# Projections put between the attention's iterations, and a quarter of the U tiles put between the V tiles

## The reference, cut to what matters

```python
(fq, fk, fv, ff, gq, gk, gv, gg, glr, mga, mgb) = jnp.split(x @ w_in, IN_SPLIT_POINTS, axis=-1)
y_fox = fox_attention(fq, fk, fv, ff + bias) @ w_out_fox      # 8 heads of 64, causal, 512 frames
o = gla_chunk_attention(gq, gk, gv, log_sigmoid(glr @ gate_up + gate_bias) / 16)   # 4 heads, chunks of 64
y_gla = (rms_norm(o) * gain * silu(gg)) @ w_out_gla
x = layer_norm(ALPHA * x + (sigmoid(mga) * y_fox + sigmoid(mgb) * y_gla) @ w_out)
# PEER: 8 heads x 16 picks for each of 512 tokens, out of 128 x 128 experts
s_top, i_top = top_k(q . sub_keys, 16)       # two halves, then the best 16 of 16 x 16 pairs
gates = softmax(best)
act = gelu(x . expert_u[picked]);  ffn = sum(act * gates * expert_v[picked])
x = layer_norm(ALPHA * x + ffn)
```

## Time and profile before

| what | value |
|---|---|
| median of three runs | 2075.17 us (2071.8 to 2093.76) |
| profiled execution, own time | 2075.27 us |
| its span, first to last instruction | 2073.5 us |
| mean granted TensorE clock | 0.954 |
| busy over the span: TensorE, VectorE, ScalarE, GpSimd | 97%, 53%, 33%, 45% |
| HBM read, written | 305.96 MB, 60.82 MB |

### The profile page before, as it was taken

How to read it: one execution, slowest core, us unless ns; L and a number is a source line. 1 busy time by engine, 2 the same in 40 slices (tenths; PEclk the granted TensorE clock), 3 DMA queues, 4 the chain that set the end, 5 groups by cost and what they waited for, 6 DMA issues and landing times.

```text
span 2073.5 us, 24488 instructions
## 1 busy us (share of the span) xinstructions
PE 2012.5 (97%) x9433; PEld 1601.0 (77%) x9433; DVE 1096.2 (53%) x2127; ACT 682.6 (33%) x1031; POOL 939.9 (45%) x502
## 2 busy tenths in 40 slices
PE   8999999999989999999999999999997999999998
PEld 5787554788777888888888888888885878787786
DVE  4001223401250199895488888600156878897787
ACT  4632222422213323333333333322332333333332
POOL 6442000344416334445333333344488888888530
PEclk9998558999989999999999999999999999999999
DMA  5221000132324234444456666654477999999983
GB/s 187 92 93 60 1 0 11 61 100 89 130 88 132 82 102 149 141 149 141 145 184 195 193 199 193 194 207 148 141 274 260 353 351 335 371 378 333 401 320 122
DMA packets 164774, 368.38 MB, mean 178 GB/s; under 512 B 15266, under 2 KB 80930, under 8 KB 164531
## 3 DMA queue, kind: packets, MB, share of 16 engines
q1 hardware_dynamic: 51264, 184.57, 25.6%
q10 hardware_dynamic: 90866, 115.06, 16.4%
q0 software_dynamic: 22528, 67.19, 8.8%
HBM read 305.96 MB, written 60.82 MB: 177 GB/s over the span
## 4 chain that ended last, share of the span: by engine, by line
PE 74%; POOL 14%; issue 4%; DVE 4%; DMA 4%; ACT 1%; SPq 0%; ACTq 0%; DVEq 0%
PE bank L403 20%; PE bank L405 20%; PE bank L404 20%; POOL weight L365 8%; POOL gat L373 6%; PE bank L645 3%; DMA act<-activation_scratch 3%; PE bank L496 2%; PE bank L518 2%; PE bank L508 1%; PE bank L533 1%; DVE acc L1110 1%; PE bank L499 1%; PE bank L541 1%; DMA gat<-in_expert_v,eidx 1%
## 5 line engine op out<-in xcount | busy, mean ns | idle before, releaser
L353 POOL TENSOR_TENSOR w_lo<-stage,w_hi 128x1024 fp32r<-128x1024 f32 x224 | 543.5, 2434 | 951.2 <-ACT w_hi L703 951.1
L403 PE MATMUL bank<-x_hi,w_lo 128*128 128x512 f32 x1376 | 543.5, 395 | 6.9 <-DVE x_lo L977 4.4
L405 PE MATMUL bank<-x_hi,w_hi 128*128 128x512 f32 x1376 | 537.7, 391 | 0.0
L404 PE MATMUL bank<-x_lo,w_hi 128*128 128x512 f32 x1376 | 537.2, 390 | 0.0
L703 ACT ACTIVATE w_hi<-stage 128x1024 fp32r<-128x1024 f32 x348 | 358.7, 1041 | 23.4 <-PE bank L405 14.2
L403 PE MATMUL bank<-w_hi,wt_lo 128*128 128x512 f32 x768 | 304.0, 396 | 31.1 <-issue 18.5
L403 PEld LDWEIGHTS bank<-x_hi,w_lo 128*128 128x128 f32 x1376 | 259.4, 189 | 61.1 <-DVE x_lo L977 5.3
L404 PE MATMUL bank<-w_lo,wt_hi 128*128 128x512 f32 x768 | 302.3, 394 | 0.0
L405 PE MATMUL bank<-w_hi,wt_hi 128*128 128x512 f32 x768 | 302.2, 393 | 0.0
L405 PEld LDWEIGHTS bank<-x_hi,w_hi 128*128 128x128 f32 x1376 | 259.3, 188 | 55.4
L404 PEld LDWEIGHTS bank<-x_lo,w_hi 128*128 128x128 f32 x1376 | 259.7, 189 | 52.6 <-issue 0.2
(11 more groups left out here) (214 smaller groups left out, 1983.4 us busy)
## 6 DMA issues: line engine op xcount, KB each, us to landing
stage<-in_expert_uT SPq DMA_DIRECT2D x128, 512.0 KB
stage<-in_expert_v SPq DMA_DIRECT2D x128, 512.0 KB
stage<-in_mix_stream SPq DMA_DIRECT2D x84, 512.0 KB
gates<-gate_scratch ACTq DMA_DIRECT2D x32, 768.0 KB
act<-activation_scratch ACTq DMA_DIRECT2D x32, 768.0 KB
activation_scratch<-act_out_a ACTq DMA_DIRECT2D x64, 256.0 KB, 2.3
activation_scratch<-act_out_b ACTq DMA_DIRECT2D x64, 256.0 KB, 2.3
gate_scratch<-gstage_a ACTq DMA_DIRECT2D x6, 2048.0 KB, 11.4
```

Source lines behind the costliest of these rows:

```text
L353: nc.gpsimd.tensor_tensor(w_lo[:, slot, 0:width], stage[:, slot % STAGE, 0:width], w_hi[:, slot, 0:width], ALU.subtract).then_inc(split_do ...
L403: mm(dst, l_lo, r_hi, start=first, stop=False)
L404: mm(dst, l_hi, r_lo, start=False, stop=False)
L405: return mm(dst, l_hi, r_hi, start=False, stop=last)
```

## The change

Two parts are changed together.

In the diff the stretches are, in this order: the numbers and the order of the stream, the banks, GpSimd's loop over the stream, TensorE's attention loop, `score_unit` and V loop, ScalarE after the U phase, and VectorE's `kdec`.

The projections gk, gq, gv0 and gv1 leave the list of projections. They become 16 pieces of 24 matmuls (`FILL`: four row blocks or columns each), and each attention iteration begins with half a piece, 12 matmuls. The attention's logits then have two banks (0 and 1) and the pieces two (2 and 7). sfx now goes straight into `kdec` through the exponential, and VectorE multiplies gk's pieces into it from PSUM.

The U tiles are in two classes. Tiles 0 to 95 (`EARLY`) are computed as before. Of the last 32, block 0 is computed in the U phase, four tiles at once: x's block 0 is the stationary operand and the four tiles are the 512 moving columns (`score_unit`, eight of them, one after each 12 early tiles). Blocks 1 to 3 of each late tile are computed in the V phase, 24 matmuls of 384 columns, before every fourth V tile; so its tile is streamed a second time. Its activations stay in SBUF (`act_out`) and are multiplied with `late_gates`. V tiles are taken in the order three early, one late. In the V phase GpSimd now makes the low part of each late U tile and of the first of each four V tiles, VectorE that of the other three V tiles. The rows gathered have 5 buffers, not 8, and are written for one tile ahead.

```diff
-GATHER = 8
-EXP_AT = {9: 0, 20: 1, 32: 2, 44: 3}
-TURN_AT = {27: 1, 39: 2, 50: 3}
-FIRST_GATE = 50
-GATE_SPAN = 48
+GATHER = 5
+EARLY = 96
+LATE = NKEY - EARLY
+RUN = EARLY * UNIT // LATE
+EXP_AT = {8: 0, 19: 1, 30: 2, 41: 3}
+TURN_AT = {25: 1, 36: 2, 47: 3}
+FIRST_GATE = 47
+GATE_SPAN = 46
-FIRST_PICK = 10
-LAST_PICK = 118
+FIRST_PICK = 8
+LAST_PICK = 120
...
+def early_place(t):
+    return t + t // RUN * UNIT
+def late_place(m):
+    return NKEY + max(0, 5 * m - 4)
+def value_place(w):
+    return NKEY + 2 + w + min(w // 4, LATE - 2)
+def is_late(w):
+    return w % 4 == 3
-def on_vector(tile):
-    return tile >= NKEY + 4
+def on_vector(place):
+    return place >= NKEY and any(place == value_place(w) for w in range(NKEY) if w % 4 != 0)
...
-        fox_bank = [bank[0], bank[1], bank[2], bank[7]]
+        fox_bank = [bank[0], bank[1]]
+        fill_bank = [bank[2], bank[7]]
-        PT_UNITS = ["fq", "fk", "z", "fv", "gk", "sfx", "gq", "tot", "gv0", "gv1"]
+        PT_UNITS = ["fq", "fk", "z", "fv", "sfx", "tot"]
+        FILL = [("gk", r) for r in range(TB)] + [("gq", r) for r in range(TB)]
+        FILL += [("gv0", r) for r in range(TB)] + [("gv1", r) for r in range(TB)]
...
-            for tile in range(2 * NKEY):
-                n, v = first_expert + tile, tile - NKEY
-                if not on_vector(tile):
-                    split_low(n, n % RING, QW)
-                while acts_due < min(NPICK, 4 * (v - FIRST_PICK + 7), picks_by(v + 3) + 2 * CHUNK_PICKS):
-                while rows_due < picks_by(v + 3):
+            for p in range(len(tiles)):
+                n = first_expert + p
+                if not on_vector(p):
+                    split_low(n, n % RING, QW)
+                w = value_at[p]
+                while acts_due < min(NPICK, 4 * (w - FIRST_PICK + 7), picks_by(w + 1) + 2 * CHUNK_PICKS):
+                while rows_due < picks_by(w + 1):
...
             for i in range(NS + 4):
+                if i < NS:
+                    fill(i)
...
-                    if i >= 4:
-                        pe.wait_ge(fox_exp, i - 3)
-                    L = fox_bank[i % 4]
+                    if i >= 2:
+                        pe.wait_ge(fox_exp, i - 1)
+                    L = fox_bank[i % 2]
...
+            def score_unit(place):
+                n = first_expert + place
+                s = n % RING
+                for k in range(UNIT):
+                    wait_split(pe, n + k)
+                dst = next_out()
+                for c in range(KC):
+                    w = slice(c * P, (c + 1) * P)
+                    ins = mm3(dst[:], x_hi[:, c, 0:P], x_lo[:, c, 0:P], w_hi[:, s:s + UNIT, w], w_lo[:, s:s + UNIT, w],
+                              c == 0, c == KC - 1)
+                ins.then_inc(quarter_used, UNIT)
...
+            score_tile(late_place(0), P)
             for v in range(NKEY - TAIL_TILES):
-                wait_split(pe, first_value + v)
+                if v % 4 == 0:
+                    score_tile(late_place(v // 4 + 1), P)
+                wait_split(pe, first_expert + value_place(v))
...
-                if t == last_group_tile + 2:
-                    load_unit(0)
-                    load_unit(1)
+            for half in range(2):
+                sc.wait_ge(gm_written[half], 16 * NGB // 2)
+            load_unit(0)
+            load_late_gates(0)
+            load_unit(1)
...
-            for r in range(TB):
-                dve.wait_ge(proj_evac, 20 + r + 1)
-                v.tensor_tensor(kdec[:, r, :], kdec[:, r, :], tmp[:, r % 2, :], ALU.mult).then_inc(kdec_ready, 1)
+                if i % 2 == 0 and 0 <= i // 2 - 1 < TB:
+                    r = i // 2 - 1
+                    v.tensor_tensor(kdec[:, r, :], fill_bank[r % 2][:], kdec[:, r, :], ALU.mult).then_inc(kdec_ready, 1)
```

More of the change, by code:

```diff
@@ L253, in build, with fill_quarters_used @@
         first_expert = first_query + HP
-        first_value = first_expert + NKEY
-        PT_UNITS = ["fq", "fk", "z", "fv", "gk", "sfx", "gq", "tot", "gv0", "gv1"]
+        tiles = stream()
+        vector_places = [p for p in range(len(tiles)) if on_vector(p)]
+        PT_UNITS = ["fq", "fk", "z", "fv", "sfx", "tot"]
         AUX = ["z", "sfx", "tot"]
-        STREAMED = [name for name in PT_UNITS if name not in AUX] + ["gg0", "gg1"]
+        FILL = [("gk", r) for r in range(TB)] + [("gq", r) for r in range(TB)]
+        FILL += [("gv0", r) for r in range(TB)] + [("gv1", r) for r in range(TB)]
+        STREAMED = ["fq", "fk", "fv", "gk", "gq", "gv0", "gv1", "gg0", "gg1"]
+        first_fill = 4 * STREAMED.index("gk")
+        def fill_quarters_used(halves):
+            used = 0
+            for h in range(halves):
+                name, r = FILL[h // 2]
+                if name == "gq":
+                    used += h % 2
+                elif r == TB - 1:
+                    used += 2
+            return used
         def wait_product(eng, name, r):
@@ L300, in _ @@
                     m += 1
[L301 to L304, removed]
+            for p, (kind, tile) in enumerate(tiles):
+                load(first_expert + p, expert_uT[tile] if kind == "u" else expert_v[tile])
             for t in range(TB):
@@ L520, in _ @@
                     ins.then_inc(fox_pv, 1)
+            quarter[0] += 16
+            pe.wait_ge(fill_evac, 3 * TB)
             pe.wait_ge(kdec_ready, TB)
@@ L946, in normalize @@
                 act_f(sd[:, t:t + 1], mv[:, t, 1:2], ACT.Sqrt, bias=eps_col).then_inc(ln2_sqrt, 1)
-            for v in range(1, NKEY):
+            units = 2
+            for v in range(NKEY):
                 round_weight(v)
-                if v + 3 < NKEY:
-                    ahead(first_value + v + 3)
-                if v % UNIT == 0 and v // UNIT + 1 < NUNIT:
+                ahead(min(first_expert + value_place(v) + 3, first_expert + len(tiles) - 1))
+                if v % 4 == 1:
+                    gelu_out(late_place(v // 4), ND)
+                if units < EARLY // UNIT and v == value_of_early(UNIT * (units - 1) - 1) + 1:
                     sc.wait_ge(wt_done, v)
-                    load_unit(v // UNIT + 1)
+                    load_unit(units)
+                    units += 1
+                if v % 16 == 15 and v + 1 < NKEY:
+                    load_late_gates(v // 16 + 1)
                 if v == LN_FIRST - 2:
@@ L1245, in split_value @@
                                 ALU.subtract).then_inc(value_split, 1)
-            for tile in range(NKEY, NKEY + 3):
-                if on_vector(tile):
-                    split_value(tile)
             weigh(0)
+            if on_vector(value_place(1)):
+                split_value(value_place(1))
             for w in range(NKEY):
```

270 lines of the change are left out of this document (184 added, 86 removed).

## The result

The changed kernel takes 2108.2 us (median of 4 runs, 2097.33 to 2114.72), the kernel before 2076.57 on the same chip: ratio 1.0115, 95% interval 1.0065 to 1.0166. The ratios are given as they were measured and are not quotients of the two medians (here 1.0152); an execution more than 1.5% above the fastest of its kernel doesn't count in them. The changed kernel is slower by 1.2%, where 2% faster was forecast, and lies above the range's end of 2078. Its profiled execution took 2097.33 us, with a span of 2095.3.

What follows compares the result with a forecast made beforehand. TensorE's own work at the lower clock was taken to bound the attention, GpSimd's gathers, just above TensorE, the V phase. 2075.3 - 50 (part one) + 8 (part two) = 2033 us, range 1998 to 2078.

Steps and rivals of the forecast that it cites:

- Part one: Attention: projections moved between its iterations let it run at full clock; -50 us, ends -60 and -35.
- the other end: Attention: upper figure, 10 us in place of 4, for 64 changes between dense and small work.
- The scan behind the attention ... runs at 1.00: Scan behind the attention: its small matmuls run at 1.00, so attention mixed with dense work should get the higher clock.
- the 16 roundings that stood ahead before: Attention, ScalarE: it gets 12 evacuations and these roundings, being busy for only 34.85 of 136.35 us before.
- Rival 3: Attention: clock does not rise, 2181 us, chance 0.03; at 0.50 for a third of the time, 2067 us, chance 0.10.
- Part two: Late tiles in U and V phases: V's losses become 54 us against 46; +8 us, between -25 and +45.
- TensorE never waits there: U phase: its 770 us are 694 us of matmuls and 76 us of 96 gate groups, without waits.
- the gate groups and turnings stand at the same times: U phase: timing of gates and turnings unchanged, since 47 early tiles and three units are 50; no cost given.
- (a): Start of V phase: GpSimd needs 79 us up to a split that TensorE reaches after 57; 20 us lost.
- (d): V phase: lower clock after the stalls at the start; 4 us lost.
- (b): V phase, after the start until near V tile 91: 20 groups at 1.1 us, GpSimd behind TensorE; 22 us lost.
- (c): Change from U to V: first gates and activations arrive late; 5.5 us of waiting and 2.5 for lower clock, 8 us.

## Why the prediction was wrong

**Part one, forecast -50, measured -17.** The clock of the attention was right, and its price nearly. Of the 179.9 us, 84 are 31 half pieces at 0.226 us a matmul, 4.5 the first one, which ran partly at the lower clock, 2.5 the two waits and 0.8 the lower clock behind them; the attention's own work is left with 80, where 82 were taken. The rest is the changes between dense and small work: a half piece takes 2.96 us from its first matmul to the next logits, where twelve at 0.226 are 2.71, so they cost 0.25 us each, 7.7 in all, 4 more than taken and within the 10 of the other end. What failed is the step "The scan behind the attention ... runs at 1.00", used as evidence for the attention and left in the sum as it was, at no cost. I had asked which clock the moved work would get, not which clock the unmoved work behind it would inherit. I also counted "the 16 roundings that stood ahead before" as hidden because ScalarE has time on the whole. They are hidden in the sum and not at the place: two of them ahead of a copy of pT, 2.0 us, are longer than the slack in the last iterations, which have no projection left. That cost 1.03 and 1.51 us of waiting and, through the clock, 30 us in the scan.

The row of the scan also had less to say than I took from it. Before, the clock rose in the attention's own tail, three microseconds ahead of the scan:

```profile
318.00:321.00 3.00, 3.00 (x12) 2.12 (x13) 1.78 (x5) 1.07 (x4) 0.00 (x0) 0.50 0.00 0
321.00:322.00 1.00, 1.00 (x6) 0.50 (x6) 0.00 (x0) 0.26 (x1) 0.00 (x0) 0.74 0.00 0
322.00:325.00 3.00, 3.00 (x23) 2.36 (x24) 0.00 (x0) 1.13 (x3) 0.00 (x0) 1.00 0.00 0
```

There TensorE turned and multiplied its last blocks without a wait, and the scan began at the level that this tail had reached. The earlier trace rows has a part of it: products with fv at 0.127 us each, the price at full clock, in a stage whose mean is 0.52. The change put waits of 1.03 and 1.51 us into just that tail.

**Rival 3,** that the clock would not rise, was near in its size, 34 us of the 50 against 33, by luck, and wrong in its place. The attention, with pieces of projections among its small matmuls from end to end, stands at 1.00. So what the Trainium skill tells in TensorE: Matmul & The Clock Gate, "A second HAM failure mode", that frequent short idling between groups makes the clock go back and forth, isn't what happened: behind two waits came one fall, and it held for 68 us of TensorE without a wait. No run here shows a clock that goes back and forth between the iterations.

**Part two, forecast +8, measured +43 alone.** "TensorE never waits there", said of the U phase and its gate groups, and that "the gate groups and turnings stand at the same times", failed: 48 us where I had nothing. Two things had changed under these sentences. The roundings of several tiles now come due together behind each unit; and the 96 groups are spread over 46 tiles in place of 48, so that three groups follow four of them. I had put the added roundings "beside other work" on ScalarE, and had not followed them to GpSimd and from there to VectorE, although show a VectorE operation of 0.57 us taking 2.45 beside a split, and I quoted it for the V phase alone.

Of the V phase's terms, (a) to (d), the sum was 54 us and 34 came, the 28 of the V window and 5.8 of waiting ahead of it. (b), GpSimd behind by 1.1 us per group, was 22 and is 0: a gather cost 1.70 us, not 1.78, which is 0.7 us on nine gathers, and the two splits 4.9 us, not 5.3. (a), the start, was 20, and with (d) it was 24; 25 were measured, 13 in the six waits and about 12 at the lower clock after them. Their kind was not the one forecast: five of the six are for weights from VectorE and one, 1.9 us, for GpSimd's split; VectorE in turn waited 55.8 us for gathered rows from 1413 to 1640 us. (c) was 8 and is right: 5.8 us of waiting and about 3 at the lower clock. The narrow matmul was taken at 0.170 us and cost 0.174.

The profiled execution is 64 us above 2033, the median 75. The windows give for it 30 for the scan, 48 for the gates, 5 because the attention gave 45 us and not 50 (its ends moved from 92.5 and 324.8 us to 93.7 and 280.5), 3 for narrow matmuls and 1 at the change of phase, less 21 that the V phase lost less than forecast (25 against 46 of (a), (b) and (d)): 66. The 11 us between the profiled execution and the median have no profile. The chance of 0.10 for slower was put on GpSimd falling behind in V, which did not happen.

## What to carry to other kernels

Work that is put into free time of an engine needs the free time at its own place: look at the last iterations of a loop, which have less cover than the mean, and at bursts in which work that was even comes due at once. Follow an added operation one engine further than the one that issues it, above all from GpSimd to VectorE. And when a stage changes TensorE's clock, price the stage behind it as well, at either level: here two waits, 2.5 us together, just ahead of the scan cost nearly its whole length again.

## What was not expected of the hardware

The scan, the same instructions, took 66.6 us at a granted clock of 0.50 or 36.8 us at 1.00, by what stood ahead of it: waits of 1.03 and 1.51 us that ended 4 and 2 us before it in the one case, none in the other. Once low, the clock stayed low for 68 us, although TensorE had no wait in it, and rose at about 347.1 us, with the first of the 512-column matmuls behind the scan.

VectorE's multiplication of two bf16 tiles took 0.36 us alone (1.08 for three) and 2.5 beside GpSimd's splits, the length of one split; a comparison ahead of it (L1393) went from 0.41 to 2.62 in the same burst. A single split costs one such delay. TensorE didn't feel it before the change, with two gate groups behind every tile; in the changed kernel it waited 3.3 us where three groups follow a tile, and 4.5 behind six splits in a row.
